# Feed-forward stage of a two-block transformer kernel: centre tap and rounding on ScalarE, idle products on TensorE in the norm transitions

## What is computed

```python
mix = jnp.concatenate([y_ssd, y_rwkv], axis=-1).astype(h.dtype) @ w_out[l]
h = h + _rms_norm(mix, post_mix_norm[l])
hn = _rms_norm(h, pre_ffn_norm[l])
u = _causal_dwconv(hn @ ffn_w_up[l], ffn_conv_w[l], ffn_conv_b[l])
gate, val = jnp.split(u, 2, axis=-1)
f = (jax.nn.silu(gate) * val) @ ffn_w_down[l]
h = h + _rms_norm(f, post_ffn_norm[l])
...
h = rms_norm(x, g_norm1[l]) * (1.0 + sc1) + sh1
```

## Time and profile before

| | us |
|---|---|
| median of three runs | 1720.13 |
| lowest, highest | 1719.09, 1734.86 |
| the profiled execution | 1716.44 |
| its span, first to last instruction | 1714.6 |
| PE busy | 1647.8 (96%) |
| VectorE busy | 1195.9 (70%) |
| GpSimd busy | 684.3 (40%) |
| ScalarE busy | 474.9 (28%) |
| chain that ended last | PE 83%, VectorE 8%, DMA 4%, ScalarE 2% |
| mean granted TensorE clock | 0.985 of full speed |

### The profile page before, as it was taken

The page is one execution under the profiler, slowest core; times in us unless marked ns, Lnnn a source line. Parts: engine busy times, 40 slices in busy tenths (PEclk is TensorE's granted clock), DMA queues, the critical chain, the costliest instruction groups (busy, mean ns, idle before and its releaser), DMA issues.

```text
span 1714.6 us, 29053 instructions
## 1 busy us (share of the span) xinstructions
PE 1647.8 (96%) x11906; PEld 1286.8 (75%) x11906; DVE 1195.9 (70%) x1609; ACT 474.9 (28%) x724; POOL 684.3 (40%) x382
## 2 busy tenths in 40 slices
PE   8999989999799999999799999999999999999998
PEld 6888577767588888888578787877878767666665
DVE  7959787756688888888674288388546426666674
ACT  4122434522220110111320132221331024544542
POOL 4765000024266666666356535345445640000000
PEclk9999999999899999999899999999999999999999
DMA  6222531131242222222222221213122256888883
GB/s 257 99 98 99 175 122 53 53 125 51 74 185 98 98 98 98 98 98 98 75 99 98 74 68 57 67 57 120 71 74 74 99 208 240 318 338 345 342 327 151
DMA packets 34070, 230.53 MB, mean 134 GB/s; under 512 B 4132, under 2 KB 4388, under 8 KB 8232
## 3 DMA queue, kind: packets, MB, share of 16 engines
q1 hardware_dynamic: 30240, 214.48, 34.4%
q10 hardware_dynamic: 2136, 10.24, 1.5%
q0 software_dynamic: 1584, 4.21, 0.7%
HBM read 220.98 MB, written 9.50 MB: 134 GB/s over the span
## 4 chain that ended last, share of the span: by engine, by line
PE 83%; DVE 8%; DMA 4%; ACT 2%; issue 1%; POOL 1%; SPq 0%; DVEq 0%; POOLq 0%; ACTq 0%
PE psum L458 82%; DVE arena L1818 2%; DMA arena<-units 2%; PE psum L462 1%; ACT arena L1406 1%; DVE arena L1824 1%; DVE in_lo L1818 1%; DMA normed<-units 1%; DVE expert_lo L1818 1%; DVE residual L1818 0%; ACT expert_hi L1406 0%; DVE arena L2502 0%; DMA arena<-x 0%; DVE smalls L2497 0%; DVE tiny L1832 0%
## 5 line engine op out<-in xcount | busy, mean ns | idle before, releaser
L1406 ACT ACTIVATE arena<-psum 128x512 f32<-128x512 f32 (+1 forms) x279 | 143.3, 529 | 751.7 <-PE psum L458 675.9
L458 PE MATMUL psum<-arena 64*64 64x64 f32 (+6 forms) x2852 | 212.5, 258 | 16.4 <-DVE arena L1818 10.0
L458 PEld LDWEIGHTS psum<-arena 64*64 64x64 f32 (+4 forms) x2852 | 142.2, 144 | 72.4 <-issue 48.3
L458 PE MATMUL psum<-normed_hi,w_in_hi 128*128 128x512 f32 x488 | 193.2, 396 | 1.0 <-ACT arena L1406 0.6
L458 PE MATMUL psum<-normed_hi,w_in_lo 128*128 128x512 f32 x488 | 190.4, 390 | 0.0
L458 PE MATMUL psum<-in_lo,w_in_hi 128*128 128x512 f32 x488 | 190.2, 390 | 0.0
L1818 DVE TENSOR_TENSOR arena<-arena,psum 128x512 f32<-128x512 f32 (+2 forms) x200 | 111.6, 588 | 100.5 <-PE psum L458 68.0
L2755 POOL TENSOR_TENSOR w_ff_lo<-weight_ring,w_ff_hi 128x1024 fp32r<-128x1024 f32 x65 | 166.9, 2568 | 5.4
L1824 DVE SCALAR_TENSOR_TENSOR arena<-arena,fixed_data 128x512 f32<-128x512 f32 x138 | 154.8, 1123 | 11.7 <-DVE arena L1821 0.2
L2755 POOL TENSOR_TENSOR w_in_lo<-weight_ring,w_in_hi 128x1024 fp32r<-128x1024 f32 x61 | 154.6, 2534 | 5.1
L2753 POOL TENSOR_SCALAR w_in_hi<-weight_ring 128x1024 fp32r<-128x1024 f32 x61 | 72.2, 1184 | 173.7 <-PE psum L458 157.7
(11 more groups left out here) (299 smaller groups left out, 3590.8 us busy)
## 6 DMA issues: line engine op xcount, KB each, us to landing
weight_ring<-units SPq DMA_DIRECT2D x124, 1024.0 KB, 4.9
arena<-units SPq DMA_DIRECT2D x55, 1024.0 KB, 7.0
normed<-units SPq DMA_DIRECT2D x20, 1024.0 KB, 8.0
slots<-arena ACTq DMA_DIRECT2D x7, 516.0 KB, 9.3
arena<-slots SPq DMA_DIRECT2D x7, 516.0 KB, 5.8
fixed_data<-fixed ACTq DMA_DIRECT2D x1, 2944.0 KB, 10.4
arena<-x SPq DMA_DIRECT2D x4, 512.0 KB, 6.0
arena<-bias_rows ACTq DMA_DIRECT2D x2, 896.0 KB, 4.5
```

The source lines that it names most:

```text
L458: return nc.tensor.matmul(o, l, r, start=start, stop=stop)
L1406: return nc.scalar.activation(o, i, func, **kw)
```

## The change

Three things.

1. In `silu_gates` ScalarE, after copying an up tile from PSUM into F_UB, reads the same bank again and forms tap 2 times the tile plus the bias (Identity with scale and bias) into F_CB; it frees the bank only then. VectorE keeps the two other taps.
2. In `finish_gate` VectorE multiplies both pairs first; ScalarE rounds each result to the high part (Copy); VectorE then subtracts both low parts. New semaphores: ffn_mul_ready, ffn_hi_ready. ScalarE no longer waits for ffn_zeroed. Elsewhere three semaphores of the state-space step are merged in two (dt_step_ready, dt_exp_ready); the instructions there stay.
3. `warm(n)` on PE issues n products of the identity by itself into bank 1, which nobody reads. Five stand ahead of each of the four waits for the root, and two ahead of each of the eight pieces of the second sums of both transitions.

```diff
+KEEP_RSTD = 5
+KEEP_SUMS = (2, 2, 2, 2, 2, 2, 2, 2)
...
+            def warm(n, b=1):
+
+                pe.wait_ge(free[b], used[b])
+                for _ in range(n):
+                    mm(PSB[b][:, 0:P], C("ident"), C("ident"))
+
+            def token_sums(what, srcs, ready, b=4, between=()):
 
                 o = open_(what, 0, b)
                 for k, src in enumerate(srcs):
+                    if k < len(between) and between[k]:
+                        warm(between[k])
                     pe.wait_ge(*ready(k))
                     for j in range(4):
                         last = mm(o[32 * j:32 * j + 32, 0:P], C("ones", P, 0, 32), src[:, j * P:(j + 1) * P],
                                   k == 0, k == len(srcs) - 1)
                 close(last, what)
...
-            def spread_rs(what, b=4):
+            def spread_rs(what, b=4, idle=0):
 
                 n_rs[0] += 1
+                if idle:
+                    warm(idle)
                 pe.wait_ge(sem("rstd_ready"), n_rs[0])
...
-            spread_rs("sum_post_mix")
+            spread_rs("sum_post_mix", 4, KEEP_RSTD)
             last_rows(0, 0)
-            sums("sum_pre_ffn", sq8, "sq_pre_ffn", 0)
-            spread_rs("sum_pre_ffn")
+            sums("sum_pre_ffn", sq8, "sq_pre_ffn", 0, KEEP_SUMS)
+            spread_rs("sum_pre_ffn", 4, KEEP_RSTD)
...
-            spread_rs("sum_post_ffn")
+            spread_rs("sum_post_ffn", 4, KEEP_RSTD)
...
-            sums("sum_1", sq8b, "sq_1", 0)
-            spread_rs("sum_1")
+            sums("sum_1", sq8b, "sq_1", 0, KEEP_SUMS)
+            spread_rs("sum_1", 4, KEEP_RSTD)
...
+                fc0 = at(j, 16, S0 + SMALL["ffn_conv"][0])
+
+                def tap(i, k):
+                    return fix[:, bass.ds(fc0 + (4 * i + k), 1)] if it is not None else \
+                        fix[:, fc0 + 4 * i + k:fc0 + 4 * i + k + 1]
+
                 for i in range(4):
                     k = (phase, sub, i)
                     if j != 0:
                         act.wait_ge(sem("ffn_taps_used"), at(j, 4, i - 3))
                     filled(act, "ffn_up", k, it)
-                    f(A(F_UB + i * PADW + 3), PSB[i], ACT.Copy).then_inc(freed("ffn_up", k), 1)
+                    f(A(F_UB + i * PADW + 3), PSB[i], ACT.Copy)
+                    f(A(F_CB + i * T), PSB[i], ACT.Identity, scale=tap(i, 2), bias=tap(i, 3)).then_inc(freed("ffn_up", k), 1)
                 for i in range(2):
                     act.wait_ge(sem("ffn_taps_used"), at(j, 4, i + 1))
                     f(A(F_CB + i * T), A(F_CB + i * T), ACT.Silu).then_inc(sem("ffn_silu_ready"), 1)
+                for i in range(2):
+                    act.wait_ge(sem("ffn_mul_ready"), at(j, 2, i + 1))
+                    f(acts.hi(2 * sub + i), acts.raw(2 * sub + i), ACT.Copy).then_inc(sem("ffn_hi_ready"), 1)
...
-            act.wait_ge(sem("ffn_zeroed"), 1)
...
-                if j != 0 and tiles[0] == 0:
-
-                    dve.wait_ge(sem("ffn_act_ready"), at(j, 2, 0))
                 for i in tiles:
                     emptied(dve, "ffn_up", (phase, sub, i), it)
                     u, c = lambda s_: A(F_UB + i * PADW + 3 - s_), A(F_CB + i * T)
-                    link(ts(c, u(0), tap(i, 2), tap(i, 3), ALU.mult, ALU.add))
                     link(stt(c, u(1), tap(i, 1), c, ALU.mult, ALU.add))
                     stt(c, u(2), tap(i, 0), c, ALU.mult, ALU.add).then_inc(sem("ffn_taps_used"), 1)
...
                     dve.wait_ge(sem("ffn_silu_ready"), at(j, 2, i + 1))
                     if i == 0:
                         dve.wait_ge(sem("ffn_taps_used"), at(j, 4, 4))
-                    link(tt(acts.raw(2 * sub + i), A(F_CB + i * T), A(F_CB + (2 + i) * T), ALU.mult))
-                    split(acts, 2 * sub + i, "ffn_act_ready")
+                    tt(acts.raw(2 * sub + i), A(F_CB + i * T), A(F_CB + (2 + i) * T), ALU.mult).then_inc(sem("ffn_mul_ready"), 1)
+                for i in range(2):
+                    q = 2 * sub + i
+                    dve.wait_ge(sem("ffn_hi_ready"), at(j, 2, i + 1))
+                    tt(acts.lo(q), acts.raw(q), acts.hi(q).bitcast(F32), ALU.subtract).then_inc(sem("ffn_act_ready"), 1)
...
-                ch.enter(it, 24)
+                ch.enter(it, 8)
```

21 lines of the change are left out of this document (10 added, 11 removed).

## The result

The changed kernel took 1710.77 us (median of 16 runs, 1706.67 to 1715.01), the kernel before 1720.09 us measured beside it (16 runs, 1715.90 to 1734.86). The medians differ by 9.3 us, a ratio of 0.9946; the ratio estimated from all runs is 0.9935, 95% interval 0.9914 to 0.9955, which is 7.7 to 14.8 us less. The forecast was 5.3 less and a time of 1714.8; the time lies in the range of 1707 to 1721 and the case "within 1%" came in, but the interval lies on the far side of the forecast. The second is settled in part: one source lies in the FFN, and some of the difference between the two profiles lies outside everything that was predicted.

What follows compares the result with a forecast made beforehand. PE was taken to bound the FFN loop, so only its edges gain: 2.7 (end) + 1.6 (transition ahead) + 1.0 (behind) = 5.3 us, giving 1714.8 us. Own range 1711 to 1719; 8 in 10 range 1707 to 1721.

Steps and rivals of the forecast that it cites:

- within 1%: Whole kernel: the time stays within 17 us of before; chance 0.95.
- The transition ahead: Norm transition before the FFN, to 465 us: clock stays up, spread 1.16 instead of 2.08 us; 1.6 us gained.
- Net 0: Last piece of second sums, transition ahead: starts some 0.2 us later but ends at full clock, so nothing lost.
- The transition behind: Norm transition after the FFN, 829 to 852 us: spread 0.9 us and first product 0.1 us faster; 1.0 us gained.
- The end of the FFN: Wait ahead of down(10), 814 to 820 us: 1.0 us shorter, plus 1.7 from no clock fall; 2.7 us gained.
- PE is at work again before the moment of the fall: End of the FFN: PE resumes 0.9 us before the clock's fall at 816.9, so no fall; 1.7 us gained.
- wait of 1.74 us: PE wait ahead of a spread, cited as one after which the clock stayed up.
- The FFN loop: nothing: Inside the FFN loop: PE is busy 25.00 of 25 us, so VectorE's saving and ScalarE's added work cost nothing.
- more than these edges: Rival: second multiply not held, end wait gone (1.7 us more), transitions at upper bounds (0.5 more); 1712.6 us, chance 0.15.
- the wait at the end stays: Rival, end of the FFN: PE stands as long, clock still falls, only transitions gain; 1717.5 us, chance 0.2.
- the idle products at half clock: Rival, both transitions: idle products fail to hold the clock and come late, 3.3 us each; 1725.7 us, chance 0.1.
- the new bound on ScalarE: Rival, FFN loop: ScalarE's longer turn makes PE wait 0.7 us in ten steps; 1721.8 us, chance 0.03.

Runs made afterwards that it cites:

- before_again: The kernel before, unchanged, run and profiled a second time; 1719.29 us, ratio to before 1.0004.
- tap_first: The kernel before plus the idle products, with ScalarE forming the centre tap in the FFN's first step alone; 1714.92 us, ratio to before 0.9945.
- tap_only: The changed kernel with the rounding of the gated activations back on VectorE, centre taps still on ScalarE; 1715.11 us, ratio to before 0.9944.
- warm_only: The kernel before with only the idle products added, nothing changed in the FFN; 1720.38 us, ratio to before 1.0014.
- warm_again: The same code as warm_only (kernel before plus idle products alone), run once more; 1721.81 us, ratio to before 1.0011.

## Why the prediction was right, and where it fell short

**The transition ahead: right.** Forecast 1.6; A-B gives 1.38 (23.60 to 22.22; 1.24 against before_again). Clock 1.00, spread at 1.16. From the second spread to the first FFN product it is 1.13 us less (3.88 to 2.75; forecast 1.1) and from there to B 0.42 less (forecast 0.5). The term "Net 0" for the late last piece was 0.17 us of loss. **The transition behind: right.** Forecast 1.0, measured 0.76 (22.50 to 21.74): 0.92 behind the spread, less 0.16 for the last piece. The 0.1 us for the first product did not come. It takes 0.47 us before and after, since the clock was already back when it began.

**The end of the FFN: right in size and mechanism.** The wait is 1.06 shorter (forecast 1.0), with the second multiply held; the rounding of the first tile lies under it and that of the second beside the first subtraction (809.91 and 810.02), as the prediction had it (the chain goes through that rounding, not through the subtraction). The clock stayed up: another 1.5 (forecast 1.7; down(10) takes 10.78 us from its first product to its last, 12.28 before). It stayed up in all five profiles with a wait of 1.48 or 1.49. The reason given, that PE is at work again before the moment of the fall, is not shown: in tap_first PE had been at work for 1.3 us (813.90 to 815.2) when the clock fell. The wait of 1.74 us that the prediction names as harmless is also not the one in its rows, where the spread runs at half rate; it is the one ahead of the first spread, which the trace of before has as well:

```profile
446.07 1.16 PE L458 MATMUL psum<-tiny,fixed_data 128*128 128x128 f32 x8 [1.74 <-ACT tiny L1406]
```

Together these make 4.70 us for the forecast 5.3. A-F is 410.03 - 405.04 = 4.99 us shorter; the other 0.29 lie between B and the last product of down(9), most of it at the two tiles of down(0) that were slightly late in before.

The forecast's range was drawn too narrow for its own terms: their bounds add up to 2.2 us more and 3.1 us less, not 1.5 on either side.

**The step that failed: "The FFN loop: nothing".** It took its cover from a steady stretch (PE 25.00 of 25, VectorE 21.55) and stretched it over the FFN's first step, where VectorE is busy 28.01 of 30 us from 500 to 530. In one of two profiles of the kernel before, and in both with the idle products added, PE waits there 2.8 us. In no profile of the changed kernel does it, so against before_again the change gives 413.32 - 405.04 = 8.28 us. Two of the three timed differences, 6.3 and 6.8 us, lie between 5.0 and 8.3; the third, 9.3, lies above both. How many of before's timed runs had the wait is not known, and in the two profiles of the result it was not there: the 4.9 us beyond A-F lie ahead of A and behind F. Of those behind F, up to 1.7 us go with the fall of the clock at 1438.1, which after does not have; whether the change has a part in that is open. So that the time landed in the range rests on the predicted terms, and that it came 4 us under the forecast has one shown source and others that are not. The only profile read for the prediction was one without the wait; its 93% of busy time was a reason to look, though, as seen above, no proof of a wait. The rival "more than these edges" came near in time (1712.6), by a mechanism that did not occur.

The rival "the wait at the end stays" fell (1.48), as did the idle products at half clock (1.00 in every profile with them) and the new bound on ScalarE: the added read took 0.77 us a tile, with PE at 25.00 of 25.

## What to carry to other kernels

An engine that is hidden in the steady loop need not be hidden in its first step; read the first and the last steps apart, and take two profiles of the kernel before to see which waits come and go. Where an instruction with two SBUF inputs stands beside GpSimd's work, moving it can give its hold to the next such instruction. The roundings moved to ScalarE took 0.63 us beside GpSimd's work, but at the end of the FFN the second multiply took over the hold. Idle products pay only where what they speed up is what the next engine waits for, and only as many as fit into the wait.

## What was not expected of the hardware

- Behind PE waits of 2.54 us ahead of down(10) the clock fell in six of six profiles, behind one of 2.34 in tap_only it did not. Behind the waits of 3.07 to 3.44 us at 585 us behind F it fell in eight of thirteen. At the start, behind the wait of 2.84 it stayed up in before_again (0.50 for the first product) and behind 2.80 it fell at once in warm_only (0.80), and a few products later in warm_again (0.66 over 520 to 525). The same code in the same place can come out either way, worth 1.5 us.
- With the idle products alone the start of the FFN was dearer: with the wait in all three, B-E is 367.32 in before_again and 368.79 and 369.13 with them. The difference is about the 1.5 us that such a fall costs at the end of the FFN. That the idle products bring the fall about is not shown; it is two profiles against one.
- Of two reads of the same bank by ScalarE, the one with scale and bias took 773 ns and the plain copy 599, as the groups above show.
